# RWKV layer: low-rank units placed between the k units, first half of the output projection placed in the last core

## The chip, the cores and the metric

The kernel runs on one core of a Trainium2 chip. The metric is the device time of one execution in microseconds (us): the median of three runs is 2372.4 (2369.59 to 2377.89).

## What is computed

The program is two transformer-like blocks over 512 tokens of width 1024. The change touches only the first layer of the first block, the RWKV time mix. Cut to what matters:

```python
xx = x_prev - x
xs = x[None] + xx[None] * mu[:, None, None, :]           # six mixed inputs: r k v w a g
rkv = jnp.einsum('nbtd,nde->nbte', xs[:3], w_rkv)
w_log = -jax.nn.softplus(-(w0 + jnp.tanh(xw @ w1) @ w2)) - 0.5
decay = jnp.exp(-jnp.exp(w_log))
a = jax.nn.sigmoid(a0 + (xa @ a1) @ a2)
g = jax.nn.sigmoid(xg @ g1) @ g2
kk = normalised per head(k * k_k);  k = k * (1 + (a - 1) * k_a)
S, y = scan over tokens:  S = S*w + (S a) b^T + v k^T;  y = S r
yn = normalised per head(y) * lnx_w + lnx_b
out = (yn + sum(r * k * r_k) * v) * g
return out @ w_o
```

Then comes `x = x + rmsnorm(m, norm_g)`, a feed-forward block, an attention layer and the second block.

## The kernel before, in words

Data lie as (128 channels of a tile, tile, token): 8 tiles of 128 channels by 512 tokens. A dense product is a list of units. One unit makes 128 output channels; it takes up to 8 k tiles, and each k tile is three matmuls of 128x128 by 128x512, because weights and inputs are split into a high part and a low remainder (`w_hi*a_hi`, `w_lo*a_hi`, `w_hi*a_lo`). Weights go through four slots: SP loads `w_raw` (L487), ACT makes `w_hi` (`high`, L574), DVE makes `w_lo` (`low`, L1022), PE uses them (L1719), and ACT or DVE reads the bank of the slot. The split of a unit is issued two units ahead (`LEAD`). Each engine walks its own list in program order and waits on counters; nothing is reordered at run time.

The mix of an input runs tile by tile over ACT, DVE, ACT, DVE: `sq` (L636), `tmp` (L1074), high part (L642), low part (L1080). PE takes k tile k of a phase once low part k is there.

The order in the RWKV layer is: `r` (8 units), with the mix for `k` beside it; `k` (8 units), with the mix for `w1` beside it; `lora`, four units w1, a1, g1 and the rest of g1. The a1 mix is made after the last k unit has been read, into the `a` operands that k used; the g1 mix after unit w1 has been read (L682 to L690), into the `b` operands. Then PE waits for all banks (`wait_evacuated`, L1765) and prepares head pair 0: `key_norms` (L1774), `decay_product` (L1778), `rate_product` (L1782), four k tiles of v, `gate_product` (L1786 and L1787), four more of v (`v_steps`, L1797), `bonus_sums` (L1805), and the first three k tiles of v for pair 1. `front` transposes four operands (L1809) and makes eight score products (L1839), which DVE masks (L1236) and from which POOL takes the off-diagonal blocks (L553).

`core(j)` runs once for each of the 8 head pairs: five levels that grow an inverse (L1861, L1880), the solve (L1906), state products (L1914 to L1944), and the carry over 8 chunks (L1959 and L1966), in which each state waits for a DVE step (L1347). In cores 0 to 6 the preparation and v steps of later pairs stand between the levels and the carry steps; core 7 has none (`core(DT - 1, False)`). After it come the normalisation of pair 7's output (L1845, L1250, L739, L1849, L745, L1254 to L1273), then the split of the eight `z_t` tiles (L794 and L1380), then the splits of the first weights of `w_o` and its eight units, each copied to `m` and squared by ACT. POOL adds the first six squares (L564), PE sums the rest (L1745), and `n_wo` ends in `std` (L589) and `rstd` (L1028). SP loads `w_o` only once all eight tiles are done.

Scratch tiles of the preparation and the cores share the space of the `a` and `b` operands and of the weight slots.

Of the kernel before, what the change touches and what calls it, by code (L numbers as in the profile page):

```python
# [26 lines left out]
P = 128  # L27
T = 512
# [67 lines left out]

def phase_list():

    out = [("r", 8, (8,) * 4), ("k", 8, (8,) * 4), ("lora", 4, (8,) * 4), ("w_o", 8, (8,) * 4)]
# [20 lines left out]
STRAIGHT = ("r", "in", "vt", "heads", "gpool", "bpool")  # L120

FENCES = ("lora",)
# [47 lines left out]
MIXES = {"r": (0, 0, "b"), "k": (1, 1, "a"), "w1": (2, 3, "b"), "a1": (3, 4, "a"), "g1": (4, 5, "b")}  # L170
# [78 lines left out]
def build(nc, dram, out_d):  # L249
    with ExitStack() as ctx:  # L250
# [60 lines left out]
        v_raw = [at(f"v_raw{i}", [P, DT, P], W0 + (20 + 2 * i) * ROW) for i in range(2)]  # L311
# [4 lines left out]
        rows_free = iter([M0 + ROW * i for i in range(8)] + [A0 + ROW * i for i in range(16)]  # L316
                         + [B0 + ROW * i for i in range(8, 16)] + [W0 + ROW * i for i in range(20)])
        half_rows = []

        def scratch(name, shape=(P, T)):  # L320

            if int(np.prod(shape[1:])) * 4 > ROW // 2:
                return at("rw_" + name, shape, next(rows_free))
            if not half_rows:
                row = next(rows_free)
                half_rows.extend((row + ROW // 2, row))
            return at("rw_" + name, shape, half_rows.pop())

        (sig_w, cum, inv_decay, a_gate, k_sq, k_norm, k_clamp, k_inv, kk, a_dec, b_tok, b_dec, k_fac, k_new,
         k_dec, r_dec, rkr, v_s) = (scratch(n) for n in (  # L330
             "sig_w cum inv_decay a_gate k_sq k_norm k_clamp k_inv kk a_dec b_tok b_dec k_fac k_new k_dec "
             "r_dec rkr v_s").split())
        a_nat, b_nat, k_nat, v_nat, x_nat, w_nat, u_nat = (
            scratch(n, (P, TT, P)) for n in "a_nat b_nat k_nat v_nat x_nat w_nat u_nat".split())
        ab, rb, ak, rk, inv, inv_t, off, prod = (
            [scratch(f"{n}{p}", (P, TT, HEAD)) for p in range(2)] for n in "ab rb ak rk inv inv_t off prod".split())
        trans, r_hat, states = scratch("trans"), scratch("r_hat"), scratch("states", (P, NCH, HEAD))
        gain = scratch("gain", (P, NCH, HEAD))

        y_t, y_dev, y_sq, y_std, y_rstd, y_n = (scratch(n) for n in "y_t y_dev y_sq y_std y_rstd y_n".split())  # L340
# [90 lines left out]

        def fixed_wait(eng):

            eng.wait_ge(const_loaded, 32)
# [38 lines left out]
        def _(sp):  # L475
# [20 lines left out]
            for name in ("r", "k", "lora"):  # L496
                load(name)
# [71 lines left out]
        def _(act):  # L569
# [108 lines left out]
            read_out("k", lambda i, r: act.activation(tile(k_t, SLOTS * i + r), bank[r][:, :], ACT.Copy), "w1")  # L678
            mix_tiles("a1")

            def read_lora(i, r, c):
                act.wait_ge(unit_done[r], c + 1)  # L682
                rows = (slice(0, 64), slice(64, P), slice(0, P), slice(0, G_REST))[r]
                dst = (lora_wa, lora_wa, lora_g0, lora_g1)[r]
                act.activation(dst[rows, :], bank[r][rows, :], (ACT.Tanh, ACT.Copy, ACT.Sigmoid, ACT.Sigmoid)[r])\
                    .then_inc(bank_free[r], 1)
                if r == 0:
                    mix_tiles("g1")
            over_units(act, "lora", read_lora, high)
# [24 lines left out]
            def prep_decay(q, first=False):  # L714
# [7 lines left out]
                act.activation(tile(z_t, q), bank[3][:, :], ACT.Copy).then_inc(ggate_ready, 1)  # L722
# [23 lines left out]

            def core(j, ahead=True):
                for lv in range(1, LEVELS + 1):
# [8 lines left out]
                    if ahead:  # L757
# [15 lines left out]
            prep_inputs(0)  # L773
            prep_norm(0)
            prep_sigmoids(0)
# [12 lines left out]
            core(DT - 1, False)  # L788
            deviation(DT - 1)
            deviation_root(DT - 1)  # L790

            act.wait_ge(tile_done, DT)
# [1571 lines left out]
```

## Time and profile before

| What | us |
|---|---|
| Median of 3 runs | 2372.4 |
| Profiled execution | 2370.42 |
| Its span | 2368.5 |
| PE busy | 2203.1 (93%) |
| DVE busy | 1308.4 (55%) |
| ACT busy | 929.1 (39%) |
| POOL busy | 99.4 (4%) |

The span runs from the first to the last instruction that the profile shows, and the execution's own time is 1.9 us longer. Stages by time in the span: `k` units 87 to 131 us, `lora` units to 167, preparation of pair 0 to 188, cores from there to 550, output of pair 7 to 570, `w_o` to 617, end of its norm (`std`) at 619.9. The mean granted clock of TensorE over the span was 0.968 of its higher level, 2.4 GHz; 0.50 is the lower one, 1.2 GHz. A busy PE is not a PE at its peak: matmuls overlap, so the time of one is read from start to start.

### The profile page before, as it was taken

The numbers are of one execution on the slowest core, as the hardware profiler recorded it, in microseconds if no ns is written. First come the engines' busy times: TensorE is split into PE (matmuls) and PEld (weight loads), VectorE is DVE, ScalarE is ACT, GpSimd is POOL, SyncE is SP. The second block draws the span as 40 slices with busy tenths as digits, with TensorE's granted clock in tenths as the row PEclk, the third lists the DMA queues.
The fourth block names the chain that finished last, engine by engine and source line by source line (L and its number), as shares of the span: only waits on it lengthen the run. The fifth ranks groups of instructions, "written<-read, shape, count | busy, mean of one in ns | idle before, by whom it ended". The sixth has DMA issues, their size and how long they took to land.

```text
span 2368.5 us, 37383 instructions
## 1 busy us (share of the span) xinstructions
PE 2203.1 (93%) x14830; PEld 1717.5 (73%) x14830; DVE 1308.4 (55%) x1978; ACT 929.1 (39%) x1471; POOL 99.4 (4%) x114
## 2 busy tenths in 40 slices
PE   4989999986899999879998999999799999999997
PEld 2856666665688888646776888888467787888886
DVE  4565777674564545584654645545654544434444
ACT  4573343332442332345654533323334444322222
POOL 0001111110000000100001000001000001000001
PEclk8989999997999999989999999999899999999999
DMA  3300000003133332201111232333120232332321
GB/s 124 98 30 27 15 18 24 6 3 122 58 107 98 97 98 91 78 27 42 40 54 63 89 106 89 100 95 90 57 71 27 63 115 84 103 98 98 98 85 66
DMA packets 53030, 168.89 MB, mean 71 GB/s; under 512 B 6920, under 2 KB 11144, under 8 KB 52768
## 3 DMA queue, kind: packets, MB, share of 16 engines
q1 hardware_dynamic: 52896, 167.00, 22.2%
q8 instruction: 96, 1.57, 0.3%
q14 instruction: 38, 0.31, 0.0%
HBM read 164.88 MB, written 2.10 MB: 71 GB/s over the span
## 4 chain that ended last, share of the span: by engine, by line
PE 83%; DVE 12%; ACT 2%; issue 1%; DMA 0%; SPq 0%; DVEq 0%; ACTq 0%
PE bank L1719 61%; PE bank L2153 2%; PE bank L1797 2%; PE bank L2046 2%; PE bank L1745 2%; PE bank L1880 1%; DVE rstd L1028 1%; PE bank L2083 1%; PE bank L2065 1%; PE bank L1861 1%; PE bank L2163 1%; DVE rw_k_inv L1172 1%; PE bank L1906 1%; DVE tmp L1057 1%; DVE tmp L1074 1%
## 5 line engine op out<-in xcount | busy, mean ns | idle before, releaser
L1719 PE MATMUL bank<-a_hi,w_hi 128*128 128x512 f32 x1424 | 571.9, 402 | 37.5 <-DVE w_lo L1022 20.1
L1719 PE MATMUL bank<-a_hi,w_lo 128*128 128x512 f32 x1424 | 558.2, 392 | 0.0
L1719 PE MATMUL bank<-a_lo,w_hi 128*128 128x512 f32 x1424 | 557.6, 392 | 0.0
L1022 DVE TENSOR_TENSOR w_lo<-w_raw,w_hi 128x1024 fp32r<-128x1024 f32 (+3 forms) x322 | 369.9, 1150 | 240.9 <-ACT w_hi L574 235.2
L574 ACT ACTIVATE w_hi<-w_raw 128x1024 fp32r<-128x1024 f32 (+3 forms) x322 | 311.4, 969 | 185.7 <-PE bank L1719 180.5
L1719 PEld LDWEIGHTS bank<-a_hi,w_hi 128*128 128x128 f32 x1424 | 269.5, 189 | 111.7 <-issue 35.1
L1719 PEld LDWEIGHTS bank<-a_hi,w_lo 128*128 128x128 f32 x1424 | 270.1, 190 | 60.0 <-issue 6.1
L1719 PEld LDWEIGHTS bank<-a_lo,w_hi 128*128 128x128 f32 x1424 | 269.6, 189 | 56.9
L1719 PE MATMUL bank<-b_hi,w_hi 128*128 128x512 f32 x640 | 254.6, 398 | 20.3 <-DVE b_lo L1080 19.7
L1719 PE MATMUL bank<-b_hi,w_lo 128*128 128x512 f32 x640 | 251.0, 392 | 0.0
L1719 PE MATMUL bank<-b_lo,w_hi 128*128 128x512 f32 x640 | 250.9, 392 | 0.0
L1719 PEld LDWEIGHTS bank<-b_hi,w_hi 128*128 128x128 f32 x640 | 121.0, 189 | 52.9 <-issue 20.4
L1719 PEld LDWEIGHTS bank<-b_hi,w_lo 128*128 128x128 f32 x640 | 121.5, 190 | 25.2 <-issue 1.0
L1719 PEld LDWEIGHTS bank<-b_lo,w_hi 128*128 128x128 f32 x640 | 121.2, 189 | 25.5
L1745 PE MATMUL bank<-sq,consts 128*128 128x512 f32 x114 | 68.6, 713 | 47.3 <-ACT sq L582 47.2
L824 ACT ACTIVATE b_hi<-tmp 128x512 f32 (+1 forms) x66 | 41.7, 632 | 172.2 <-DVE tmp L1420 172.2
L815 ACT ACTIVATE gconv<-gpad,vecs 128x512 f32<-128x512 f32 x44 | 35.9, 817 | 184.0 <-DVE gpad L1405 184.0
L553 POOL TENSOR_TENSOR rw_off<-rw_ab,consts 128x256 f32<-128x256 f32 x80 | 60.4, 769 | 471.1 <-DVE rw_ab L1236 351.5
L564 POOL TENSOR_TENSOR gconv<-sq,sq 128x512 f32<-128x512 f32 x6 | 7.8, 1296 | 1693.3 <-ACT sq L582 1693.3
L1745 PEld LDWEIGHTS bank<-sq,consts 128*128 128x128 f32 x114 | 23.0, 220 | 76.3 <-issue 51.0
L1424 DVE TENSOR_TENSOR b_lo<-tmp,b_hi 128x512 f32 (+1 forms) x66 | 45.7, 692 | 57.1 <-ACT b_hi L824 57.1
L1797 PE MATMUL bank<-v_mix,v_raw 128*128 128x512 f32 (+1 forms) x164 | 75.4, 558 | 0.0
(312 smaller groups left out, 3027.7 us busy)
## 6 DMA issues: line engine op xcount, KB each, us to landing
w_raw<-in_f0gu SPq DMA_DIRECT2D x44, 512.0 KB, 3.5
w_raw<-in_f1gu SPq DMA_DIRECT2D x44, 512.0 KB, 3.5
w_raw<-in_f2gu SPq DMA_DIRECT2D x44, 512.0 KB, 3.5
w_raw<-in_f0dn SPq DMA_DIRECT2D x16, 512.0 KB, 3.5
w_raw<-in_f1dn SPq DMA_DIRECT2D x16, 512.0 KB, 3.5
w_raw<-in_f2dn SPq DMA_DIRECT2D x16, 512.0 KB, 3.5
w_raw<-in_in SPq DMA_DIRECT2D x10, 512.0 KB, 3.6
w_raw<-in_r SPq DMA_DIRECT2D x8, 512.0 KB, 6.3
```

The costliest lines, as they stand in the source:

```text
L553: pool.tensor_tensor(off[p][:, :, :], ab[p][:, :, :], mask, ALU.mult).then_inc(off_ready, 1)
L574: act.activation(w_hi[r][:, 0:n, :], raw[r][:, 0:n, :], ACT.Copy).then_inc(w_high[r], 1)
L815: act.activation(gconv[:, :], gpad[:, 2:T + 2], ACT.Identity, scale=column(vecs, base + 2, 4 * ft), bias=column(vecs, base + 3, 4 * ft))\
L824: act.activation(tile(opnd["b"][0], 2 * i + r // 2), tmp[(r // 2) % 2][:, :], ACT.Copy)\
L1022: dve.tensor_tensor(w_lo[r][:, 0:n, :], raw[r][:, 0:n, :], w_hi[r][:, 0:n, :].bitcast(F32), ALU.subtract).then_inc(w_split[r], 1)
L1028: dve.reciprocal(rstd[:, :], std[:, :]).then_inc(rstd_ready, 1)
L1424: dve.tensor_tensor(tile(opnd["b"][1], t), tmp[par][:, :], tile(opnd["b"][0], t).bitcast(F32), ALU.subtract).then_inc(bank_free[r], 1)
L1719: mm = pe.matmul(bank[r][:, :], w[r][:, k, :], a[:, k, :], start=(k == 0 and n == 0), stop=(k == kt - 1 and n == 2))
L1745: mm = pe.matmul(bank[7][:, :], const("ones"), source[:, :], start=(j == j0), stop=(j == n - 1))
L1797: mm = pe.matmul(bank[V_BANK][:, lo:hi], v_raw[q % 2][:, k, :], v_mix[:, k, lo:hi], start=(k == 0 and lo == 0), stop=(k == DT - 1), skip_g ...
L2046: mm = pe.matmul(bank[u % 2][:, :], w[r][:, k, :], a[:, k, :], start=(k == 0 and n == 0), stop=(k == HEAD_TILES[u % 3] - 1 and n == 2))
L2153: mm = pe.matmul(bank[v % 2][:, :], w[r][:, k, :], a[:, k, :], start=(k == 0 and n == 0), stop=(k == KS[name][0] - 1 and n == 2))
```

## The change

`k` and `lora` become one phase `kl` of 12 units in which the low-rank units stand between k units. All three low-rank mixes go into the `b` operands, in groups of two to four tiles, each after ACT has read a given unit. Key norms, decay product and rate product of pair 0 are issued inside the last two units. PE then waits for the banks of those two alone, and the two first v loads are released earlier. The first three v tiles of pair 1 stand between the scores of `front(0)`.

In core 7, `z_t` tiles 0 to 6 are split level by level, the first weights of `w_o` are loaded and split, and PE takes k tiles 0 to 5 of `w_o` unit 0 in the carry. K tile 6 and the first seven k tiles of units 1 to 3 stand around and behind the mean and variance of pair 7; k tile 7 of these four units follows, then units 4 to 7. Scratch tiles are laid out anew so that slots and operands are free in time; the decay and gate products of pair 0 use bank 4 in place of 3; units 0 to 7 of `w_o` use the banks in `WO_BANK`.

```diff
+WO_BANK = (5, 6, 0, 1, 2, 3, 4, 5)
+FIRST_V = ((1, 0), (1, 2), (0, 2))
+KL = ("k", "k", "k", "w1", "k", "k", "k", "a1", "k", "k", "g1", "g1")
+KL_MIXES = {-1: ("w1", 0, 3), 0: ("w1", 3, 6), 1: ("w1", 6, 8), 3: ("a1", 0, 3), 4: ("a1", 3, 6), 5: ("a1", 6, 8),
+            7: ("g1", 0, 4), 8: ("g1", 4, 8)}
-    out = [("r", 8, (8,) * 4), ("k", 8, (8,) * 4), ("lora", 4, (8,) * 4), ("w_o", 8, (8,) * 4)]
+    out = [("r", 8, (8,) * 4), ("kl", len(KL), (8,) * 4), ("w_o", 8, (8,) * 4)]
...
 SP
+                    if name == "w_o" and i == 0 and r == 2:
+                        sp.wait_ge(y_inner, DT)
-            wait_evacuated(sp, "lora")
+            for r in range(2):
+                sp.wait_ge(unit_done[r], START["kl"][r] + 3)
             load_v(0)
             load_v(1)
...
+            load("w_o")
             sp.wait_ge(tile_done, DT)
-            load("w_o")
...
 ACT (DVE has the same groups with mix_tmp_of and mix_low_of)
-            mix_tiles("a1")
+            def mix_group(at_unit):
+                if at_unit not in KL_MIXES:
+                    return
+                phase, lo, hi = KL_MIXES[at_unit]
+                mix_base_of(phase, lo, lo % 2)
+                for j in range(lo, hi):
+                    if j + 1 < hi:
+                        mix_base_of(phase, j + 1, (j + 1) % 2)
+                    mix_high_of(phase, j, j % 2)
+            def read_kl(i, r, c):
+                u = SLOTS * i + r
...
+                mix_group(u)
+                if u == 9:
+                    prep_inputs(0)
+                    prep_norm(0)
+                    prep_decay_sigmoid(0)
+                elif u == 10:
+                    prep_rate_sigmoid(0)
+            def split_high(j):
+                act.wait_ge(scored, DT * 8)
+                act.wait_ge(tile_done, j + 1)
+                act.activation(opnd["a"][0][:, j, :], z_t[:, j, :], ACT.Copy).then_inc(z_high, 1)
 ACT, core 7, after level lv
+                        split_high(lv - 1)
+                        if lv in (2, 3):
+                            ahead_of(high, WO + lv - 2)
 ACT, core 7, after w_nat
+                    split_high(5)
+                    split_high(6)
 ACT, after core 7
+            ahead_of(high, WO + 2)
             deviation(DT - 1)
+            ahead_of(high, WO + 3)
             deviation_root(DT - 1)
+            split_high(DT - 1)
+            for u in range(UNITS["w_o"]):
+                r, c = u % SLOTS, START["w_o"][u % SLOTS] + u // SLOTS
+                if u + SLOTS < UNITS["w_o"] + LEAD:
+                    ahead_of(high, WO + u + SLOTS)
+                act.wait_ge(unit_done[r], c + 1)
+                act.activation(m[:, u, :], bank[WO_BANK[u]][:, :], ACT.Copy).then_inc(bank_free[r], 1)
+                act.wait_ge(bank_free[r], c + 1)
+                square("n_wo", lambda j: m[:, j, :], u)
...
 DVE, core 7, after level lv
+                        split_low(lv - 1)
+                        if lv in (2, 3):
+                            dve.wait_ge(v_done, DT)
+                            ahead_of(low, WO + lv - 2)
 DVE, core 7, before the gain step, and after the states
+                    split_low(5)
+                    split_low(6)
 DVE, after core 7
+            ahead_of(low, WO + 2)
+            ahead_of(low, WO + 3)
             for n in range(4):
                 output_root(DT - 1, n)
...
 DVE, preparation of pair 0: the scan stands ahead of the reciprocals
+            prep_cum(0)
             for n in range(4):
                 prep_inverse(0, n)
-            prep_cum(0)
...
 PE
+            def kl_unit(u):
...
+                for k in range(DT):
+                    if (u, k) == (10, 4):
+                        key_norms(0)
+                        kl_evacuated(pe, 3)
+                        decay_product(0)
+                    elif (u, k) == (11, 4):
+                        kl_evacuated(pe, 7)
+                        rate_product(0)
+                    if KL[u] != "k" or u == 0:
+                        pe.wait_ge(mix_low, MIXES[KL[u]][0] * DT + k + 1)
...
 PE, front, ahead of score (p, n)
+                    if q == 0 and (p, n) in FIRST_V:
+                        v_steps(1, (FIRST_V.index((p, n)),))
 PE, core, carry step ch
+                        if not ahead:
+                            w_o_steps(0, (ch - 1,))
...
+            for u in range(len(KL)):
+                kl_unit(u)
+            kl_evacuated(pe, 10)
+            kl_evacuated(pe, 11)
             v_steps(0, range(4))
             gate_product(0)
             v_steps(0, range(4, DT))
             bonus_sums(0)
-            v_steps(1, range(V_EARLY))
             front(0)
...
             core(DT - 1, False)
+            w_o_steps(0, (6,))
             mean_of(DT - 1)
+            w_o_steps(1, range(2))
             variance_of(DT - 1)
-            pe.wait_ge(tile_done, DT)
-            dense("w_o", ...)
+            w_o_steps(1, range(2, 7))
+            for u in (2, 3):
+                w_o_steps(u, range(7))
+            for u in range(4):
+                w_o_steps(u, (7,))
+            w_o_steps(4, range(4))
...
+            for u in (6, 7):
+                w_o_steps(u, range(8))
+                sum_squares("n_wo", u - 2)
+            sum_squares("n_wo", 6)
+            sum_squares("n_wo", 7)
```

`w_o_steps(u, steps)` waits for the weight split of its unit and, k tile by k tile, for `z_low`, and issues the three matmuls of the k tile into `bank[WO_BANK[u]]`. The number of matmuls, of weight loads and of transfers of the whole program is the same before and after.

## Rows read from the trace of the kernel before

**Rows 1.** The page, part 4: shares of the chain that ended last.
```profile
PE 83%; DVE 12%; ACT 2%; issue 1%; DMA 0%; SPq 0%; DVEq 0%; ACTq 0%
```

**Rows 2.** Timeline of ACT: start us, duration, line, tiles, idle before.
```profile
93.28 0.60 ACT L678 ACTIVATE k_t<-bank 128x512 f32<-128x512 f32 x1 [1.22 <-PE bank L1719]
...
131.36 0.60 ACT L678 ACTIVATE k_t<-bank 128x512 f32<-128x512 f32 x1 [1.83 <-PE bank L1719]
```

**Rows 3.** Waits of PE, 84 to 200 us: total us, times, longest.
```profile
PE bank L1719 <- DVE b_lo L1080: 4.7, 3, 4.1
PE bank L1719 <- DVE a_lo L1080: 2.8, 7, 0.4
PE bank L1774 <- ACT rw_k_sq L698: 1.4, 1, 1.4
PE bank L1861 <- POOL rw_off L553: 1.0, 1, 1.0
PE bank L1870 <- DVE rw_ak L1236: 0.9, 1, 0.9
```

**Rows 4.** Timeline of PE, columns as in the ACT timeline: preparation and first scores.
```profile
131.16 0.39 PE L1719 MATMUL bank<-b_hi,w_hi 128*128 128x512 f32 x1
...
168.79 1.10 PE L1774 MATMUL bank<-rw_k_sq,consts 128*128 128x512 f32 x2 [1.38 <-ACT rw_k_sq L698]
...
172.50 6.21 PE L1797 MATMUL bank<-v_mix,v_raw 128*128 128x512 f32 x8
...
180.55 3.70 PE L1797 MATMUL bank<-v_mix,v_raw 128*128 128x512 f32 x8
...
185.03 2.81 PE L1797 MATMUL bank<-v_mix,v_raw 128*128 128x512 f32 x6
...
187.68 0.60 PE L1809 MATMUL bank<-consts,rw_a_dec 128*128 128x128 f32 x4
...
198.43 1.98 PE L1797 MATMUL bank<-v_mix,v_raw 128*128 128x512 f32 x4
```

**Rows 5.** Timeline of ACT: a weight split, then the mix ahead of a1.
```profile
128.49 1.05 ACT L574 ACTIVATE w_hi<-w_raw 128x1024 fp32r<-128x1024 f32 x1
...
133.92 1.32 ACT L636 ACTIVATE sq<-hp,one_minus_mu 128x512 f32<-128x512 f32 x2
...
137.85 0.61 ACT L642 ACTIVATE a_hi<-tmp 128x512 fp32r<-128x512 f32 x1
...
144.68 0.63 ACT L642 ACTIVATE a_hi<-tmp 128x512 fp32r<-128x512 f32 x1 [0.76 <-DVE tmp L1074]
```

**Rows 6.** Windows: length, busy PE, PEld, DVE, ACT, POOL; granted clock, DMA.
```profile
151.00:157.00 6.00, 5.83 (x13) 3.70 (x14) 5.82 (x10) 5.66 (x10) 0.00 (x0) 0.50 0.00 0
...
524.00:540.00 16.00, 15.18 (x268) 14.57 (x268) 7.08 (x18) 2.90 (x7) 2.77 (x5) 0.50 0.01 2
...
550.50:570.50 20.00, 4.15 (x4) 1.01 (x4) 12.79 (x19) 8.18 (x14) 0.00 (x0) 0.50 0.27 94
```

**Rows 7.** Waits of PE, 510 to 630 us.
```profile
PE bank L1719 <- DVE w_lo L1022: 13.7, 1, 13.7
...
PE bank L1959 <- DVE rw_states L1347: 1.4, 5, 0.3
```

**Rows 8.** Chain of waits in order of time: start us, us, what.
```profile
545.54 0.34 PE bank L1959 x4
...
549.91 0.50 PE bank L1966 x4
...
557.57 3.40 DVE rw_y_rstd L1254 x4
...
563.02 0.70 DVE z_t L1273
...
570.55 39.76 PE bank L1719 x168
...
619.17 0.69 ACT std L589
```

More of the change, by code:

```diff
@@ L333, in build, with scratch @@
-        a_nat, b_nat, k_nat, v_nat, x_nat, w_nat, u_nat = (
-            scratch(n, (P, TT, P)) for n in "a_nat b_nat k_nat v_nat x_nat w_nat u_nat".split())
-        ab, rb, ak, rk, inv, inv_t, off, prod = (
[L336 to L340, printed above, removed]
+        def scratch(rows, name, shape=(P, T)):
+            half = int(np.prod(shape[1:])) * 4 <= ROW // 2
+            if half and rows["half"] is not None:
+                offset, rows["half"] = rows["half"], None
+            else:
+                offset = rows["free"].pop(0)
+                rows["half"] = offset + ROW // 2 if half else rows["half"]
+            return at("rw_" + name, shape, offset)
@@ new lines, in region @@
+        def region(*spans):
+            return {"free": [base + ROW * i for base, lo, hi in spans for i in range(lo, hi)], "half": None}
+        prep_rows = region((A0, 0, 16))
+        core_rows = region((W0, 4, 8), (W0, 12, 16), (W0, 20, 24))
+        kept_rows = region((M0, 0, 8), (B0, 8, 16))
+        (sig_w, cum, inv_decay, a_gate, k_sq, k_norm, k_clamp, k_inv, kk, a_dec, b_tok, b_dec, k_fac, k_new,
+         k_dec, rkr) = (scratch(prep_rows, n) for n in (
+             "sig_w cum inv_decay a_gate k_sq k_norm k_clamp k_inv kk a_dec b_tok b_dec k_fac k_new k_dec rkr").split())
@@ L341, in build @@
+        states, gain = (scratch(kept_rows, n, (P, NCH, HEAD)) for n in "states gain".split())
+        y_t, y_dev, y_sq, y_std, y_rstd, y_n = (scratch(kept_rows, n) for n in "y_t y_dev y_sq y_std y_rstd y_n".split())
         decay = at("decay", [P, NCH, CHUNK + 1], G0)
@@ L788, in _ @@
             core(DT - 1, False)
+            ahead_of(high, WO + 2)
             deviation(DT - 1)
+            ahead_of(high, WO + 3)
             deviation_root(DT - 1)
-            act.wait_ge(tile_done, DT)
-            for j in range(DT):
-                act.activation(opnd["a"][0][:, j, :], z_t[:, j, :], ACT.Copy).then_inc(z_high, 1)
-            start_ahead(high, "w_o")
-            square_units("w_o", "n_wo", lambda j: m[:, j, :],
-                         lambda i, r: act.activation(tile(m, SLOTS * i + r), bank[r][:, :], ACT.Copy))
+            split_high(DT - 1)
[7 more added lines that the diff above has]
+                square("n_wo", lambda j: m[:, j, :], u)
+            root_mean("n_wo")
             late_norm("n_f0", "f0", x_updated("w_o"))
@@ L1715, in body @@
                             inside(r, k)
-                        if ready is not None and (r == 0 or name == "lora"):
+                        if ready is not None and r == 0:
                             ready(r, k)
@@ L1800, in v_steps, with w_o_steps @@
                     mm.then_inc(v_done, 1)
+            def w_o_steps(u, steps):
+                r, c = u % SLOTS, START["w_o"][u % SLOTS] + u // SLOTS
+                hi, lo = opnd["a"]
+                for k in steps:
+                    if k == 0:
+                        pe.wait_ge(w_split[r], c + 1)
+                        if u == 0:
+                            pe.wait_ge(vs_ready, DT)
+                        elif u == 7:
+                            pe.wait_ge(bank_free[0], START["w_o"][0] + 1)
+                    pe.wait_ge(z_low, k + 1)
+                    for n, (w, a) in enumerate(((w_hi, hi), (w_lo, hi), (w_hi, lo))):
+                        mm = pe.matmul(bank[WO_BANK[u]][:, :], w[r][:, k, :], a[:, k, :], start=(k == 0 and n == 0),
+                                       stop=(k == DT - 1 and n == 2))
+                if k == DT - 1:
+                    mm.then_inc(unit_done[r], 1)
             def bonus_sums(q):
```

147 lines of the change are left out of this document (84 added, 63 removed).

## The prediction

> **What bounds the kernel now.** I read the page's chain first: PE holds 83% of it, and L1719, the matmuls of dense units, 61% [rows 1]. No work is removed by the change, so it can gain only where PE stands still or runs at its lower clock inside the RWKV layer. Next I read PE's waits in the two stretches that are rearranged, then the timelines and the granted clock there.
>
> The price of a unit comes first. ACT reads k unit 0 at 93.28 and k unit 7 at 131.36 [rows 2]: 38.08/7 = 5.44 us for each unit of 24 matmuls, 0.68 us for each k tile at the full clock.
>
> In the entry PE waits for mixes, not for DMA: 4.7 us on b_lo (4.1 at one time), 2.8 on a_lo, 1.4 on k_sq, and in the first scores 1.0 + 0.9 [rows 3]. After the 4.1 us of idle time the granted clock is 0.50 for 151 to 157 [rows 6]. The first v steps start at 172.50, and four k tiles take 6.21 us where the next four take 3.70 [rows 4]; the engine had gaps just before, so I read these as steps at the lower level.
>
> In the exit PE has almost nothing between 549.91 and 570.55: it waits for the normalisation of pair 7, eight z splits and two weight splits, and 13.7 us of it are one wait on w_lo [rows 7, 8]. Granted clock 0.50, PE busy for 4.15 of 20 us [rows 6]. w_o then begins at 570.55 and std at 619.17 [rows 8].
>
> **Entry, part by part.** The k units end where w1 begins, at 131.16 [rows 4], so they begin at 131.16 - 8x5.44 = 87.6.
>
> 1. Mix groups. ACT starts the a1 mix at 133.92 and finishes its third high part at 137.85 + 0.61 = 138.46, so a group of three holds ACT 4.5 us; a further tile is (144.68 - 137.85)/5 = 1.37 us [rows 5]. Between groups ACT owes a weight split, 1.05 (0.04 more to the next) [rows 5], and a read, 0.5 to 0.6 [rows 2]. A unit with a group of three so costs ACT 6.1 us against PE's 5.44, one with two 4.7, one with four 7.5. I walk this from the end of r (ACT free at 91.1: 87.6 plus the read and the last mix for k, which hold ACT 3.5). Groups -1, 0 and 1 end on ACT at 95.5, 101.5 and 106.1; the split of unit 3 is done at 103.8 and PE wants it at 103.9. Groups 3 to 5 end at 125, before a1 begins at 125.7. Groups 7 and 8 start at 131.6 and 139.0, and the last high part of g1 is there at 144.9. All w1, a1 and g1 waits then vanish but for tenths. What hides the mixes are k units; the cover ends at unit 10.
>
> 2. The new wait. Behind group 8 stand the split of unit 11, the read of unit 9, and k_sq (0.7): 144.9 + 1.05 + 0.5 + 0.7 = 147.2. PE is at k tile 4 of unit 10 at 87.6 + 10x5.44 + 4x0.68 = 144.7. It waits 2.5 us in key_norms, and the rest of unit 10, unit 11 and everything else queue behind it. Then PE: key norms 1.0 (a pass of 512 columns, 1.10 as recorded [rows 4]), decay product 1.0, 4x0.68 = 2.7 to the end of unit 10 (151.9), unit 11 with the rate product 6.4 (158.3), the read of its bank 1.0, and v can start at 159.3. DVE's chain for pair 0 (scan, reciprocals, keys) is ready at about 163, under the v steps. At full clock three v steps take 187.68 - 185.03 = 2.65, 0.88 each [rows 4]; eight v, two gate and one bonus product at that price are 9.7, and 0.4 for their ends, 10.1, so scores can start at 169.4. Before, v of pair 1 began at that point, 185.03 [rows 4]. Gain 15.6.
>
> 3. First v of pair 1: 2.65 us (185.03 to 187.68) leave the path. The masks on DVE, not the scores, set the pace there, and the steps fill 1.0 + 0.9 of waiting [rows 3]. Gain 1.9.
>
> 4. The clock. A stall of 4.1 us was followed by 6 us at the lower level [rows 3, 6]. The new one, 2.5 us, lies between that and the waits of about 1 us in the scores, which are followed by full-speed v steps (4 records, 1.98 us, at 198.43) [rows 4]. I take the drop, priced at half of those 6 us: 3.0. It is 0 if the clock holds and up to 5 if the single-pass products fall into it too. Entry: 15.6 + 1.9 - 3.0 = **14.5**, range 11 to 18.
>
> **Cores 0 to 6** keep their instructions. The moved scratch tiles and bank 4 for bank 3 add no instruction; no row shows a cost of an address, so 0, with -1 to +1 kept.
>
> **Exit, part by part.**
>
> 1. Levels of core 7. ACT gets five z copies and two w_hi, about 5 us; DVE five z_low of 0.6 and two w_lo of 1.2, 5.5. From 524 to 540 DVE is busy 7.08 and ACT 2.90 of 16 us, and PE 15.18 at clock 0.50 [rows 6]: PE at its lower clock is the bound, so the additions lie beside it. A DVE operation behind its first inverse step of levels 2 and 3 may delay the next by 0.1 to 0.3 us: 0.3 lost. If the clock were at its upper level, DVE and ACT would come near the path; the levels would still be shorter than now.
>
> 2. Carry. It runs from 545.54 to 549.91 + 0.50, six steps with 0.3 us of DVE wait each [rows 7, 8], 0.72 apart. A k tile of w_o (0.68) fills that wait; a step becomes 0.13 + 0.68 + 0.13 = 0.94. The carry ends 1.2 us later with 4.1 us of w_o done.
>
> 3. Pair 7's output. y is done at 551.6. ACT does y_t, w_hi of unit 2, the square, w_hi of unit 3, the root. The copies stand where ACT waits for the mean and the variance. On DVE two w_lo stand ahead of the reciprocals, the second ends at about 557.3; before, the reciprocals began at 557.57 [rows 8]. So z tile 7 is done at about 563.5, as at 563.02 + 0.70 now, and its split at 564.7. PE has from 551.6 mean and variance (2.0) and 22 k tiles (15.0) that don't need it, until 569. So nothing waits for z tile 7: this is the stall that goes. SP's loads of units 2 and 3 wait for y_inner (about 545); with 4 us of flight they land near 550, before ACT wants them at 552.4.
>
> 4. End. From 551.6: 58 k tiles at 0.68 = 39.4, mean and variance 2.0, 0.5 of waits, and 0.4 where the split of unit 4 waits for unit 0's last k tile (its split can start at 569.7, PE arrives at 571.7). Unit 7 ends at 593.9. Three sums behind it, the last after copy and square: 2.9, so std at 596.8 in place of 619.17 [rows 8]. Gain 22.4, less the 0.3: **22.1**, range 18 to 28.
>
> **Sum.** 2370.4 - 14.5 - 22.1 = 2333.8 against the profiled execution. The median of the runs is 2.0 above that execution, so 2336.
>
> **A rule of the skill against it.** PE stands 0.3 us before five of the carry's steps, and k tiles of w_o are to fill these gaps [rows 7, 8]. The Trainium skill, TensorE: Matmul & The Clock Gate, section A second HAM failure mode: psum-queue depth-cycling, says that small idles between groups of matmuls can make the clock oscillate. By it the new order, with a semaphore at every k tile, would run partly at 1.2 GHz; by the rows it is open, since none shows w_o inside the carry; the price of its worst case stands with the fourth rival.
>
> **Rivals.**
>
> - Mixing binds the entry. For it: ACT needs 6.1 us beside 5.44 in three-tile groups, and two groups of four in a row. If each group held ACT a microsecond more, k_sq would come 6 to 8 us later, PE would stand that long in unit 10, at the lower clock after. Against: rows 5 are such a run already. Time 2336 + 8 = 2344. Chance 0.14.
> - The exit fills worse: splits of core 7 hit DVE on the path, or part of w_o runs at the lower level (price 0.68 per k tile, 12 tiles = 8 us). For it: the clock is at 0.50 from 524 to 542. Against: the carry has its clock back. 2344. Chance 0.12.
> - Core 7 keeps its full clock, because something in timing shifts. Levels bound by the chain near 2.9 in place of 3.8 us over three of them, solve and state products 2.5 less: 5 to 6 us. 2330. Chance 0.08.
> - Slower than before. The mechanism is the clock: PE stays at 1.2 GHz from the stall in unit 10 and again through w_o. 64 k tiles of w_o cost 43.5 more, the 12 tiles after the stall 8, the v, gate and bonus work of pair 0 about 9: 60 in all, 3 of them already counted. 2336 + 57 = 2393. It passes the time before from (2372.4 - 2336)/0.68 = 54 slow k tiles on, and 0.3% above it from 64 on. For it: the same matmuls at 0.50 in 151 to 157. Against: that stretch returned to full speed within 6 us while PE was 97% busy. By the skill's rule above this is the outcome at its worst. Chance 0.03.
> - It doesn't do what it says: some wait (a slot, a bank, SP behind y_inner) puts the same idle time back, 2372. A queue position gives at most part of it. Chance 0.03.
>
> The forecast has 0.60, own range 2330 to 2342. A measurement of this kernel tells about 0.3%, 7 us, from no change. Faster by more 0.94, within 0.03, slower 0.03. Range for 8 in 10: 2324 to 2350, which takes in the first three rivals.
>
> **What would show it.** Between 87 and 152 PE has no wait on b_lo or a_lo over 0.5 us, and one on k_sq of 2 to 3 us; clock 0.50 behind it for some 5 us. The first v step starts near 162 to 163. core(0) begins 14 to 17 us earlier. In core 7 clock 0.50 from about 507 on, levels 3.8 us as now. Carry of 5.9 us. No wait on w_lo over 1 us before w_o unit 4, clock 1.00 from the carry to n_wo. From the first L1959 of core 7 to std 51.3 us in place of 73.6. The forecast is wrong if the lower clock reaches into w_o, if the stall in unit 10 exceeds 5 us, or if DVE is late with z tile 7.

## The result and the profile after

The changed kernel takes 2339.49 us (median of 4 runs, 2335.52 to 2340.12) against 2374.55 of the kernel before (4 runs). The ratio is 0.9847, interval 0.9825 to 0.9868: faster by 1.5%, 35 us. It was measured again later on another occasion (e10 below): 2338.71 of 5 runs, 0.9845, 0.9820 to 0.9870. The prediction was 2336. The two profiled executions lie 31.3 us apart (2370.42 and 2339.14), because that of before was a low one among its runs; what follows explains those 31 us, stage by stage.

The page of the changed kernel: busy times of the engines, the granted clock in 40 slices, the chain by engine. PE's busy time has hardly moved (before: 2203.1); its share of the chain is 84% against 83 [rows 1].

```profile
PE 2195.9 (94%) x14830; PEld 1715.4 (73%) x14830; DVE 1308.1 (56%) x1978; ACT 926.3 (40%) x1470; POOL 100.9 (4%) x114
...
PEclk8999999989999999899999999999899999999999
...
PE 84%; DVE 12%; ACT 2%; issue 1%; DMA 0%; SPq 0%; DVEq 0%; ACTq 0%
```

Waits of PE in the changed kernel, 84 to 200 us (total, times, longest). The waits on b_lo, a_lo and for the first scores [rows 3] are gone. One on k_sq is left.

```profile
PE bank L1868 <- ACT rw_k_sq L732: 2.2, 1, 2.2
PE bank L1891 <- issue: 0.7, 1, 0.7
PE bank L1880 <- ACT rw_sig_w L744: 0.3, 1, 0.3
PE bank L1876 <- ACT rw_k_norm L740: 0.2, 1, 0.2
```

Timeline of PE around it (start, duration, line, tiles, idle before), to be held against [rows 4]. Key norms and decay product take 2.08 and 2.07 us, twice a rate product later in the same list. v starts at 162.13 in place of 172.50, and both halves of it run at 3.7 us where the first took 6.21.

```profile
146.41 2.08 PE L1868 MATMUL bank<-rw_k_sq,consts 128*128 128x512 f32 x2 [2.23 <-ACT rw_k_sq L732]
148.41 2.07 PE L1872 MATMUL bank<-lora_wa,lora 64*128 64x512 f32 x2
...
157.32 1.12 PE L1876 MATMUL bank<-lora_wa,lora 64*128 64x512 f32 x2
...
162.13 3.67 PE L1891 MATMUL bank<-v_mix,v_raw 128*128 128x512 f32 x8 [0.72 <-issue]
...
167.64 3.70 PE L1891 MATMUL bank<-v_mix,v_raw 128*128 128x512 f32 x8
...
172.04 0.60 PE L1920 MATMUL bank<-consts,rw_a_dec 128*128 128x128 f32 x4
...
180.98 0.27 PE L1974 MATMUL bank<-rw_inv,rw_off 64*64 64x64 f32 x1
...
183.95 1.98 PE L1891 MATMUL bank<-v_mix,v_raw 128*128 128x512 f32 x4
```

Windows of the changed kernel, columns as in [rows 6]. The clock is at 0.50 behind the stall on k_sq, dips to 0.72 behind the carry of core 6, is at 0.50 in the levels of core 7, and then, unlike 550.5 to 570.5 in [rows 6], stays at 1.00 while PE works on w_o (1.00 over 543 to 588 as a whole).

```profile
144.00:147.00 3.00, 0.77 (x2) 0.50 (x2) 2.23 (x4) 2.98 (x5) 0.00 (x0) 0.87 0.56 229
147.00:152.00 5.00, 5.00 (x8) 1.80 (x7) 1.19 (x2) 3.22 (x4) 0.00 (x0) 0.50 0.01 3
495.00:500.00 5.00, 5.00 (x49) 3.89 (x48) 1.29 (x4) 2.67 (x6) 0.05 (x1) 0.72 0.00 0
515.00:520.00 5.00, 4.03 (x78) 3.92 (x76) 4.93 (x8) 2.23 (x4) 1.47 (x3) 0.50 0.01 3
535.00:538.00 3.00, 3.00 (x25) 2.01 (x25) 0.85 (x3) 0.00 (x0) 0.00 (x0) 1.00 0.81 254
```

Three of PE's waits from core 7 to the end of the norm; the 13.7 us on w_lo of [rows 7] are 0.4.

```profile
PE bank L1974 <- DVE rw_inv L1359: 3.7, 4, 1.6
PE bank L1983 <- DVE rw_ak L1300: 0.9, 1, 0.9
PE bank L1908 <- DVE w_lo L1077: 0.4, 1, 0.4
```

I cut both executions, and later those of the experiments, at the same instructions. The cuts are: first k matmul (k0), first v matmul (v0), first level matmul of core 0 (z0) and of core 7 (z7), first carry matmul of core 7 (c), ACT's y_t after it (y), std, end. In us, each column a difference of two starts in the timelines:

```
                  k0   k0-v0  v0-z0  z0-z7   z7-c   c-y   y-std  std-end    span
before          87.64  84.86  20.67  322.08  30.29  4.89  68.74  1749.33  2368.5
after           86.89  75.24  18.85  322.51  31.18  8.00  45.28  1749.35  2337.3
e1 units last   86.56  88.17  18.85  322.97  31.21  8.00  45.31  1749.43  2350.5
e2 exit plain   87.46  75.21  18.85  323.00  28.79  4.76  69.42  1754.21  2361.7
e3 bare carry   87.50  75.33  18.85  320.45  30.98  5.04  51.72  1754.93  2344.8
e4 filler       86.40  72.11  18.85  322.40  27.98  8.01  45.25  1750.30  2331.3
e5 norms later  86.91  69.59  18.85  324.03  30.26  8.01  45.30  1754.25  2337.2
e6 in levels    87.56  73.64  18.85  319.93  30.47  7.44  42.10  1749.71  2329.7
e7 first v back 87.55  75.26  18.12  329.46  30.05  8.01  45.30  1754.45  2348.2
e8 e5 and e6    85.56  69.59  18.84  322.70  28.24  7.46  42.06  1749.85  2324.3
e9 e8, filler   86.90  69.59  18.85  322.74  27.43  7.46  42.09  1748.84  2323.9
e10 after       86.50  75.20  18.85  322.50  31.17  8.00  45.28  1749.30  2336.8
```

Of the 31.2 us of span, 9.6 come between k0 and v0, 1.8 between v0 and z0, and 23.5 behind y_t. Core 7 gives back 0.9 in its levels and 3.1 in its carry, z0 to z7 0.4. The rest, 0.8, lies ahead of k0, where nothing was changed.

### The profile page after: what moved, and what is told of

Its sections match the earlier page's. It is cut to its first block, busy times and chain, and to the rows that moved or that the text cites. A ratio compares the mean times of both kernels' runs of the same rounds, so it can differ in the third digit from the quotient of the medians.

```text
span 2337.3 us, 37349 instructions
## 1 busy us (share of the span) xinstructions
PE 2195.9 (94%) x14830; PEld 1715.4 (73%) x14830; DVE 1308.1 (56%) x1978; ACT 926.3 (40%) x1470; POOL 100.9 (4%) x114
## 4 chain that ended last, share of the span: by engine, by line
PE 84%; DVE 12%; ACT 2%; issue 1%; DMA 0%; SPq 0%; DVEq 0%; ACTq 0%
PE bank L1797 58%; PE bank L2286 3%; PE bank L1857 2%; PE bank L1891 2%; PE bank L2179 2%; PE bank L1908 2%; PE bank L1823 2%; DVE rstd L1083 1%; PE bank L2216 1%; PE bank L2198 1%; PE bank L1993 1%; PE bank L1974 1%; PE bank L2296 1%; DVE rw_k_inv L1236 1%; PE bank L2019 1%
## 5 line engine op out<-in xcount | busy, mean ns | idle before, releaser
L1797 PE MATMUL bank<-a_hi,w_hi 128*128 128x512 f32 x1288 | 516.5, 401 | 21.2 <-DVE a_lo L1123 14.6
L1797 PE MATMUL bank<-a_hi,w_lo 128*128 128x512 f32 x1288 | 504.0, 391 | 0.0
L1797 PE MATMUL bank<-a_lo,w_hi 128*128 128x512 f32 x1288 | 503.8, 391 | 0.0
L1797 PEld LDWEIGHTS bank<-a_hi,w_hi 128*128 128x128 f32 x1288 | 243.6, 189 | 85.6 <-issue 18.9
L1797 PEld LDWEIGHTS bank<-a_hi,w_lo 128*128 128x128 f32 x1288 | 244.0, 189 | 54.6 <-issue 5.6
L1797 PEld LDWEIGHTS bank<-a_lo,w_hi 128*128 128x128 f32 x1288 | 243.4, 189 | 51.4
L1797 PE MATMUL bank<-b_hi,w_hi 128*128 128x512 f32 x616 | 243.0, 395 | 15.0 <-DVE b_lo L1135 14.9
L1797 PE MATMUL bank<-b_hi,w_lo 128*128 128x512 f32 x616 | 240.5, 390 | 0.0
L1797 PE MATMUL bank<-b_lo,w_hi 128*128 128x512 f32 x616 | 240.4, 390 | 0.0
L1797 PEld LDWEIGHTS bank<-b_hi,w_lo 128*128 128x128 f32 x616 | 116.2, 189 | 24.7 <-issue 1.0
L1083 DVE RECIPROCAL rstd<-std 128x512 f32<-128x512 f32 x13 | 43.6, 3352 | 62.1 <-ACT std L607 62.1
```

The source lines that it names most:

```text
L1083: dve.reciprocal(rstd[:, :], std[:, :]).then_inc(rstd_ready, 1)
L1797: mm = pe.matmul(bank[r][:, :], w[r][:, k, :], a[:, k, :], start=(k == 0 and n == 0), stop=(k == kt - 1 and n == 2))
```

## The experiments

e3 to e7 were executed once each, so that their totals (2346.62, 2333.19, 2339.11, 2331.57 and 2350.11 us) say little by themselves; I compare their stages.

**e1: low-rank units last.** The exit and the first v steps stay.

```diff
-KL = ("k", "k", "k", "w1", "k", "k", "k", "a1", "k", "k", "g1", "g1")
+KL = ("k",) * 8 + ("w1", "a1", "g1", "g1")
-KL_MIXES = {-1: ("w1", 0, 3), 0: ("w1", 3, 6), ... 7: ("g1", 0, 4), 8: ("g1", 4, 8)}
+KL_MIXES = {**{u - 1: ("w1", u, u + 1) for u in range(8)}, 7: ("a1", 0, 8), 8: ("g1", 0, 8)}
...
-  "a1": (3, 4, "b")
+  "a1": (3, 4, "a")
...
```

> Only the place of the low-rank units is undone: eight k units, then w1, a1, g1, g1, with the mixes as before the change (w1 beside k, a1 and g1 in one piece each). Exit and first v steps stay. Theory (the entry gain is mixing hidden under k units): PE waits again for the a1 and g1 mixes, about 2.8 us in small pieces and about 4 us in one, plus 3 us at the lower clock behind it; from the first k matmul to the first v step 85 us where the changed kernel has 75.2. Median about 10 us above the changed kernel, near 2349. Rival (the entry gain comes from the earlier v loads and the products inside the last units, not from the places): within 3 us of the changed kernel.

2351.68 us (4 runs), 0.9907 of before (0.9883 to 0.9931): 12 us above the changed kernel. k0 to v0 is 88.2 us, even more than the 84.9 of before. PE's waits, 84 to 200 us:

```profile
PE bank L1867 <- ACT rw_k_sq L731: 5.4, 1, 5.4
PE bank L1856 <- DVE b_lo L1134: 4.5, 2, 4.1
PE bank L1856 <- DVE a_lo L1134: 1.5, 4, 0.4
```

The waits on b_lo are back as in [rows 3], those on a_lo at about half their length, and the stall on k_sq is 5.4 us, because g1's mix and unit 11's split stand before k_sq on ACT. So the early v loads and the products inside the last units bring nothing by themselves, and the gain is gone without the new places of the units. The rival falls. What the early loads and products add once the units have their new places, no run shows.

**e2: plain exit.** The entry stays.

```diff
 SP:  load("w_o") behind sp.wait_ge(tile_done, DT) again
 ACT, DVE:  all split_high / split_low behind pair 7's output, then the units' splits, two ahead
-  w_o_steps(0, (ch - 1,))            # in the carry
-  w_o_steps(0, (6,)) ... w_o_steps(u, range(7))
+  mean_of(DT - 1)
+  variance_of(DT - 1)
+  for u in range(8): w_o_steps(u, range(DT)), sums one unit behind
```

> Only the exit is undone: z splits, weight splits, w_o loads and all w_o units come after pair 7's output again; the new entry stays. Theory: from the first carry matmul of core 7 to std 73.6 us as before the change (the changed kernel has 53.3), levels of core 7 back from 31.2 to 30.3 us; median about 19.5 us above the changed kernel, near 2359. Rival (entry and exit gains are not additive, or the clock gives part of either back): 12 us or less, or 24 and more.

2363.46 us (10 runs), 0.9957 (0.9942 to 0.9973), 24 us above the changed kernel by the medians. By the stages c to std is 74.2 us, against 53.3 in the changed kernel and 73.6 before. The old wait returns with its old length:

```profile
PE bank L1891 <- DVE w_lo L1070: 13.7, 1, 13.7
```

The median is at the edge of the rival's range (24 and more). The stages come near the 19.5 us (74.2 + 28.8 against 53.3 + 31.2 is 18.5); 4.9 more of the profiled execution lie behind std, where the two programs are alike. There e2, e3, e5 and e7 have 1754 us, and the others 1749 to 1750. The place is the same in all four: some 13 us at a granted clock of 0.50 about 601 us behind std (1208.5 to 1222 in e2, 1192 to 1205 in e3, 1184 to 1197 in e5, 1195 to 1208 in e7), where the other eight traces have 1.00. Why these four have it is open. Such a dip is worth as much as most edits here, so I read single executions by stages only.

**e3: bare carry.**

```diff
-                        if not ahead:
-                            w_o_steps(0, (ch - 1,))
-            w_o_steps(0, (6,))
+            w_o_steps(0, range(7))
```

> K tiles 0 to 5 of w_o unit 0 are taken out of the carry of core 7 and issued in one piece behind it. My prediction said that a k tile fills the 0.3 us wait of a carry step, and each step would be 0.94 us; it is 1.27 in the changed kernel. Theory A (in the carry a k tile costs 0.55 on the path, so it saves only 0.13 of its 0.68): the carry takes 4.9 us again, y_t comes 3.1 us earlier, std 1 us later or the same as now. Theory B (the tiles in the carry keep the clock up): the clock falls after the carry and std comes 3 us or more later. Theory C (the carry is better left alone): std earlier by up to 1 us, since the reciprocals start 3 us earlier and nothing else changes.

The carry takes 5.0 us, y_t to std 51.7: c to std is 56.8 in place of 53.3, std 3.5 us later, as theory B has it. Windows of e3; the first lies in its bare carry (533.1 to 538.2), in the other two PE is busy all the time:

```profile
535.00:538.00 3.00, 2.01 (x30) 1.42 (x28) 1.55 (x5) 0.00 (x0) 0.00 (x0) 0.74 1.00 393
538.00:541.00 3.00, 3.00 (x9) 2.39 (x8) 0.17 (x1) 1.60 (x3) 0.00 (x0) 0.50 0.61 247
541.00:544.00 3.00, 3.00 (x10) 2.31 (x9) 0.00 (x0) 0.00 (x0) 0.00 (x0) 0.62 0.00 0
```

The changed kernel has 1.00 there. Six k tiles moved behind the carry cost 4.1 us and save 3.0 in it; the other 2.4 are the stretch at the lower clock, 0.51 over 536.4 to 543.3. This is one execution, but the other traces agree. The two other kernels with a bare carry have the fall at the same point: before the change 1.00 over 545.5 to 549.5 and 0.50 over 549.6 to 556, e2 0.71 over 538.1 to 541 and 0.50 over 541 to 546, there with PE idle for part of the time behind the carry. All nine traces with w_o in the carry have 1.00 from y_t to std.

**e4: filler in the levels of core 7.**

```diff
+                    if not ahead:
+                        pe.wait_ge(vs_ready, DT)
+                        for _ in range(2 if lv == 1 else 1):
+                            pe.matmul(bank[V_BANK][:, :], const("ones"), v_mix[:, 0, :], start=True, stop=True)
```

> Six idle products of 128x128 by 128x512 in f32 (0.88 us each at full clock) are added to the levels of core 7, two in the first and one in each other; their result is overwritten, nothing reads it. Theory (core 7 falls to 0.50 because its levels lack the v steps that cores 0 to 6 have): the granted clock stays at 1.00 through core 7 and the stretch from its first level matmul to its first carry matmul falls from 31.2 us to 27 to 28.5, in spite of 5.3 us of added PE work. Rival (the fall has another cause, or the path there is DVE): clock 0.50 as now and the stretch grows to 34 us or more.

z7 to c falls from 31.2 to 28.0 us with 5.3 us of useless work added. (The six executions without this filler and with the same splits take 30.05 to 31.21, so the gain is 2.1 to 3.2 us.) Windows of e4: the stall on k_sq, what follows it, and a stretch in the levels of core 7.

```profile
144.00:147.00 3.00, 1.09 (x3) 0.33 (x3) 1.83 (x3) 2.98 (x4) 0.00 (x0) 1.00 0.43 175
147.00:152.00 5.00, 5.00 (x20) 3.56 (x20) 2.62 (x4) 3.33 (x5) 0.00 (x0) 1.00 0.01 3
...
515.00:520.00 5.00, 5.00 (x112) 3.88 (x113) 4.16 (x9) 2.51 (x6) 2.40 (x2) 1.00 0.02 3
```

The clock stays at 1.00 through core 7. What the filler does there is twofold, and no run separates the two. It adds wide products, and it fills idle time: the changed kernel stands 0.50 + 1.59 us in level 2, just before the clock falls, and is busy for 2.74 of the 5.00 us of 505 to 510; e4 stands 0.25 and is busy for 4.72. That the clock stayed low afterwards was not for want of busy time, since PE is busy for 4.90 of 5.00 us at 0.50 in 520 to 525 of the changed kernel.

The first two rows hold a second finding: the same stall of 2.2 us, after the same instructions, did not lower the clock in this execution, and k0 to v0 is 72.1 us in place of 75.2. That difference is the price of the drop. e6 lies between them: 0.71 in its window 147 to 152, and 73.6 us.

**e5: key norms and decay product later.**

```diff
-                    if (u, k) == (10, 4):
+                    if (u, k) == (11, 0):
```

> Key norms and decay product of pair 0 stand ahead of k tile 0 of unit 11 in place of k tile 4 of unit 10, so that 2.7 us of matmuls stand between PE and k_sq. Theory (the stall on k_sq is 2.2 us and drops the clock, which costs 3.1 us more: the run with filler kept its clock there by chance and took 72.1 us where the changed kernel took 75.2): no wait on k_sq above 0.5 us, clock 1.00 from 144 to 158, and from the first k matmul to the first v step 70 to 71 us. Rival (the later decay product makes the chain of DVE late instead): 73 us or more, or a new wait before the bonus product.

k0 to v0 is 69.6 us, 5.6 less than in the changed kernel and 2.5 less than in e4. No wait on k_sq is left. Windows of e5 (its 2339.11 us hold the dip of 1184 to 1197 us and a longer z0 to z7):

```profile
144.00:147.00 3.00, 3.00 (x14) 2.42 (x13) 2.24 (x4) 2.98 (x5) 0.00 (x0) 1.00 0.62 250
147.00:152.00 5.00, 5.00 (x17) 2.76 (x16) 1.99 (x3) 3.72 (x5) 0.00 (x0) 1.00 0.00 0
```

**e6: w_o in the levels.**

```diff
+LEVEL_SPLITS = {1: (0,), 2: (1,), 3: (2, 3), 4: (4, 5), 5: ()}
 ACT, DVE:  unit 0's weights split in core 6, unit 1's in level 4; z tiles by LEVEL_SPLITS
+                    elif not ahead and lv > 1:
+                        w_o_steps(0, LEVEL_SPLITS[lv - 1])
-                            w_o_steps(0, (ch - 1,))
+                            w_o_steps(1, (ch - 1,) if ch < NCH - 2 else ())
```

> K tiles 0 to 5 of w_o unit 0 stand in levels 2 to 5 of core 7 (1, 1, 2, 2), where the filler stood, its weights are split in core 6, and the carry takes k tiles 0 to 4 of unit 1. Theory (the levels lack work of full array width, so the clock falls): clock 1.00 through core 7, first level matmul to first carry matmul 27 to 28.5 us (31.2 in the changed kernel, 28.0 with filler), carry 7 to 8 us, y_t to std 41 to 42.5 us because five or six k tiles fewer are left; sum 76 to 78.5 in place of 84.5. Rival (the first level has no filler here and the clock falls before level 2 starts its tile): clock 0.50 in the levels, each k tile costs its whole 0.7 to 1.3 us, stretch 33 to 35 us, sum 83 or more.

z7 to std is 80.0 us, against 84.5 in the changed kernel and 76 to 78.5 expected. z7 to c is 30.5: six k tiles (4.1 us of work) at no cost, but not the 28 I expected. Windows of e6:

```profile
505.00:510.00 5.00, 3.41 (x63) 3.14 (x59) 4.93 (x10) 1.29 (x3) 1.28 (x2) 0.75 0.00 0
510.00:515.00 5.00, 5.00 (x69) 4.19 (x68) 3.13 (x9) 1.80 (x4) 1.27 (x2) 0.50 0.01 3
515.00:520.00 5.00, 4.95 (x71) 3.98 (x70) 2.99 (x8) 2.44 (x5) 1.27 (x2) 0.73 0.00 0
```

The clock falls in level 2, behind the waits of 0.50 and 1.59 us there and ahead of its k tile at 509.25, and is back by 520, within the levels. Both theories had a part of it: the fall came before the first k tile, as the rival says, but the clock came back.

**e7: first v steps ahead of the scores again.**

```diff
-                    if q == 0 and (p, n) in FIRST_V:
-                        v_steps(1, (FIRST_V.index((p, n)),))
+            v_steps(1, range(V_EARLY))
             front(0)
```

> The first three v steps of pair 1 stand ahead of the first scores again; all else is the changed kernel. Theory (they fill 1.0 and 0.9 us of waiting for off and ak): from the first v step of pair 0 to the v step in level 1 of core 0, 23.7 us in place of 21.8, and these two waits are back. Rival (they only move): 21.8 us.

PE's waits, then windows of e7:

```profile
PE bank L1972 <- POOL rw_off L571: 1.0, 1, 1.0
PE bank L1981 <- DVE rw_ak L1300: 0.9, 1, 0.9
```

```profile
184.00:187.00 3.00, 2.79 (x58) 2.79 (x58) 0.36 (x2) 1.01 (x2) 0.07 (x1) 0.59 0.02 5
187.00:190.00 3.00, 3.00 (x15) 1.64 (x14) 1.30 (x5) 0.19 (x1) 0.00 (x0) 0.50 0.00 0
```

The two waits are back with their old lengths. The first v step of pair 0 to the v step of level 1 is 24.7 us, where 23.7 were expected and the changed kernel has 21.8. The extra microsecond, and 1.9 us more from that v step to the first level matmul of core 1 (44.07 in place of 42.18), are the lower clock, 0.50 over 185 to 191: here it fell after these 1.9 us of waiting. In the kernel before it did not, after the same waits.

**e8: e5 and e6 together.**

> The two edits of e5 and e6 in one kernel, to see whether they beat the changed kernel. If both theories hold the stages add: 4 to 5 us of the entry (3 of them only in executions where the clock falls at k_sq) and 6 to 8.5 of the exit, so 10 to 13 us under the changed kernel: median 2327 to 2330, against 2374.7 of the kernel before a ratio of 0.980. If neither does, within 3 us of 2339.5.

2330.18 us (5 runs, 2326.15 to 2336.14), 0.9818 (0.9795 to 0.9841). The stages add, and a little more: k0 to v0 is 69.6 as in e5, z7 to std 77.8 where e6 has 80.0, 12.3 us less than the changed kernel together. The 2.2 us under e6 go with the clock in the levels, which is back at 1.00 by 510 here (0.66 in 505 to 510) and only by 520 in e6. The median is 9 us lower.

**e9: e8 with filler where the clock still fell.**

```diff
...
+                    elif not ahead:                      # level 1 of core 7
+                        for _ in range(2):
+                            pe.matmul(bank[V_BANK][:, :], const("ones"), v_mix[:, 0, :], start=True, stop=True)
...
+                        elif ahead:                      # carry of core 6
+                            pe.wait_ge(vs_ready, DT)
+                            pe.matmul(bank[V_BANK][:, 0:T // 2], const("ones"), v_mix[:, 0, 0:T // 2],
+                                      start=True, stop=True)
```

> e8 plus idle f32 products whose result is overwritten: two of 512 columns in level 1 of core 7 and one of 256 columns in each of the six carry steps of core 6, the places without work of full width. Theory (the clock falls in core 7 and behind the carry of core 6 only because PE lacks such work there): clock 1.00 from 470 us to std, first level matmul to first carry matmul 27 us or less (28.2 and 30.5 in e8 and e6), cores 0 to 6 (first level matmul of core 0 to that of core 7) 320 to 321 us, and no longer 322.5 to 324 in some executions; median 2 to 4 us under e8. Rival (the idle products cost as much as the clock returns): median within 1 us of e8 or above.

2326.39 us (5 runs, 2325.19 to 2332.3), 0.9806 (0.9780 to 0.9832). Windows of e9, from the cores to the carry of core 7:

```profile
200.00:470.00 270.00, 256.14 (x4953) 179.26 (x4952) 193.78 (x419) 98.70 (x178) 43.70 (x59) 1.00 0.07 20
470.00:480.00 10.00, 8.96 (x232) 6.91 (x228) 9.62 (x19) 6.05 (x11) 1.87 (x2) 1.00 0.01 3
480.00:500.00 20.00, 18.27 (x372) 13.83 (x372) 12.56 (x31) 6.00 (x11) 2.84 (x4) 1.00 0.01 2
500.00:530.00 30.00, 28.50 (x637) 22.77 (x638) 20.45 (x45) 8.84 (x18) 4.49 (x7) 1.00 0.13 40
```

No dip is left from 200 to 530 us, and z7 to c is 27.4. But z0 to z7 is 322.7 and not 320: from the first level matmul of core 6 to that of core 7 it is 47.1 us in e9 without a dip and in e8 with one, and 44.4 in e6 with neither dip nor filler. So the six products in that carry cost about what they give back. Level 1's two bring 0.8 against e8. The median lies 3.8 us under e8, inside the spread of both. e9 is the fastest version, 12 us under the changed kernel measured beside it; that it beats e8 isn't shown.

**e10: the changed kernel again, beside e9.**

> The changed kernel once more, unaltered, on the same chip as e9, so that the two are compared side by side: median 2337 to 2341, a ratio to the kernel before of 0.983 to 0.987. Its profile shows what differs from execution to execution of one program: by my theory the stall on k_sq stays at 2.2 us, and only the stretches behind stalls change with the clock, by 2 to 5 us each.

2338.71 us (5 runs). Its stages from k0 on repeat those of the first profile within 0.1 us. The changes of 2 to 5 us that I expected between executions of one program did not show in this pair.

## Why the prediction was right, and where it was off

*Entry.* Predicted: PE stands 2.5 us at key norms, the clock drops at a price of 3.0, v0 at 159.3 + 3.0 = 162.3. Measured: 2.2, 3.1 (e4 against the changed kernel), 162.13. From the first v step to that of level 1 the terms give 10.1 + (198.43 - 187.68) + 2.65 - 1.9 = 21.6; measured 21.8. To the v step of level 1 of core 0 the change gains 198.43 - 183.95 = 14.5, the predicted number; but 0.8 of it lies before k0, where nothing was changed, so the rearrangement itself gave 13.7 and the exact hit is luck. The first level matmul of core 0 comes only 12.2 us earlier (193.17 to 180.98), because the waits of 1.0 and 0.9 us that are gone had stood behind it, so the sign "14 to 17 us earlier" holds for the v step alone. e1 shows that the place of the units is the cause, e7 the part of the first v steps.

*Cores 0 to 6.* Predicted 0. From the v step of level 1 of core 0 to z7 it takes 2.7 us longer (319.5 against 316.8). That was not in the prediction. 2.5 of them lie between the first level matmuls of core 6 and core 7 (46.87 against 44.38), and their place is the window 495 to 500 at 0.72, behind the carry of core 6, which has no v steps; e3 and e6 had no such dip (320.5 and 319.9 from z0), e10 had it, and the profiled execution of before, with the same bare carry in core 6, has 1.00 over 178 to 515. The address changes have no part that could be seen.

*Levels of core 7.* The prediction put 0.3 us; it was 0.9, with the clock at 0.50 for some 20 us in both. The sign "0.50 from about 507 on" came later: 505 to 510 still has 1.00. PE now waits for DVE's transposes in levels 3 and 4, 0.65 and 0.97 us. DVE of the changed kernel:

```profile
514.78 1.13 DVE L1343 TENSOR_TENSOR a_lo<-z_t,a_hi 128x512 fp32r<-128x512 f32 x1
515.84 1.67 DVE L1077 TENSOR_TENSOR w_lo<-w_raw,w_hi 128x1024 fp32r<-128x1024 f32 x1
517.43 0.28 DVE L1355 TENSOR_TENSOR rw_inv_t<-bank,rw_inv_t 128x128 f32<-128x128 f32 x1
```

The low part of the second z tile took 1.13 us where others take 0.63, w_lo then 1.67 in place of 1.2, and the inverse step of level 3 stood behind both. The high part had been there since 512.1, so this was no wait for ACT; both ran beside POOL's rw_off (514.53 and 515.79), and why they were slower no run isolates. I had counted DVE's work against its idle share in [rows 6], and not against the moment at which the chain wants it.

*Carry.* The step "a step becomes 0.13 + 0.68 + 0.13" was mis-sized. A step is 1.27 us. Timeline of PE in the changed kernel:

```profile
534.67 0.33 PE L2072 MATMUL bank<-rw_gain,rw_trans 64*64 64x64 f32 x4
534.93 0.50 PE L1908 MATMUL bank<-a_hi,w_hi 128*128 128x512 f32 x1
535.27 0.39 PE L1908 MATMUL bank<-a_hi,w_lo 128*128 128x512 f32 x1
535.50 0.40 PE L1908 MATMUL bank<-a_lo,w_hi 128*128 128x512 f32 x1
535.82 0.33 PE L2081 MATMUL bank<-rw_r_hat,rw_gain 64*64 64x64 f32 x4
535.99 0.28 PE L2072 MATMUL bank<-rw_states,rw_trans 64*64 64x64 f32 x4
```

From the carried product to the first w_o matmul it is 0.26 (0.21 in the later steps), 0.34 to the second, 0.23 to the third, 0.32 from there to the y product, and 0.17 to the next carried one. That is 0.33 more than my 0.94, and it lies at the changes between 64x64 products in f32 and 128x128 in split form: 0.34 and 0.32 where matmuls within a k tile stand 0.23 apart, so that the k tile takes 0.89 in place of 0.68, and 0.21 and 0.17 where I had 0.13. So the carry takes 8.0 us in place of 6.1. Its 0.3 us waits did go. Bare, it is 3 us shorter, and yet e3 is slower, for a reason that I hadn't priced: with w_o in the carry the clock stayed at 1.00 in all nine traces, and with a bare one it fell in all three.

*End.* ACT's y_t, last z copy, first m copy and std:

```profile
542.67 0.66 ACT L769 ACTIVATE rw_y_t<-bank 128x256 f32<-128x256 f32 x2 [12.96 <-PE bank L2081]
...
554.32 0.63 ACT L788 ACTIVATE a_hi<-z_t 128x512 fp32r<-128x512 f32 x1 [6.45 <-DVE z_t L1337]
...
561.84 0.58 ACT L849 ACTIVATE m<-bank 128x512 f32<-128x512 f32 x1
...
587.95 0.69 ACT L607 ACTIVATE std<-bank,consts 128x512 f32<-128x512 f32 x1 [1.32 <-PE bank L1823]
```

z tile 7's high part is there at 554.9, and the copy of w_o's first finished unit stands at 561.84, after PE had worked through 28 k tiles that don't need tile 7: it was never late, and the normalisation is hidden as predicted. From y done to std was 45.2 by my walk (596.8 - 551.6); y_t to std is 45.3. c to std is 53.3 where I had 51.3, the 2 us of the carry. The exit, z7 to std, gives 103.92 - 84.46 = 19.5 us in place of 22.1, and e2 comes near it with 18.5. e2's levels are at the lower clock for 17 us (512 to 529), where the changed kernel's are for 20, and that is a part of the difference.

*The sum.* 14.5 + 19.5 - 2.7 = 31.3 in the profiled pair, against 36.6. That the medians are 35.1 apart, near the predicted 2372.4 - 2336 = 36.4, is luck and not merit of the walk: executions of one program spread over 2 to 14 us. The spread goes with the mean granted clock: of the 13 executions of the kernel before beside e1, the shortest (2366.14) has 0.968 and the longest (2379.9) 0.964.

*The rivals.* Mixing didn't bind the entry. Of the exit that fills worse one half came true, on a small scale: splits did hit DVE on the path in levels 3 and 4; no part of w_o ran at the lower level. The one that had core 7 keep its full clock is reached only with added work (e4, e9). The slow one did not occur: behind the carry PE runs w_o at 1.00. The rule cited there is that small idles between groups of matmuls make the clock oscillate (the Trainium skill, TensorE: Matmul & The Clock Gate, A second HAM failure mode: psum-queue depth-cycling). The trace agrees in the bare carry, 0.3 us of idle time per step and then 0.50 in 538 to 541 of e3. So here the rule speaks for this change rather than against it: waits at every k tile did no harm, since the weights and z tiles were there.

*Open.* Why the clock fell after one stall of 2.2 us and not after its twin (e4), and after 1.9 us in e7 and not before the change. No run here varied only that. Open too are what puts the dip behind std into four executions, and whether the filler in core 7 works by its width or by the idle time that it fills.

## What to carry to other kernels

Price a stall at its own length plus the stretch at the lower clock that may follow, here 2.2 us plus 3, and look for stages where PE does small products only, with waits between them: full-width work there, even useless work, shortened this one. When work is moved into a chain, check it against the moment at which each engine is wanted and not against idle shares, and allow for the gaps between kinds of matmul. Compare versions that are a few microseconds apart by equal cuts of the timeline, since one dip of the clock outweighs them.

## What the runs showed of the hardware that I had not expected

PE busy for 95% of the time with 64x64 products stayed at the lower clock for 16 us (524 to 540, 0.50 in [rows 6]); with one f32 product of 128x128 by 512 columns in each level, two in the first, it never fell (e4). Useless work of 5.3 us made that stage 2.1 to 3.2 us shorter. And a fall of the clock behind a given stall is not certain: of the executions with a 2.2 us stall on k_sq, five have k0 to v0 at 75.2 to 75.3, one 73.6 and one 72.1.
